# Branch units of a hybrid decoder step: each weight chunk for three token tiles in turn, instead of tile by tile

## The reference, cut to what matters

```python
z = h @ w_in
u, q, k, v, ga, gb = jnp.split(z, IN_SPLITS, axis=-1)
...
br_a = a @ w_a                                # pooling branch, 512 -> 1024
br_b = o.reshape(B, T, ATTN_WIDTH) @ w_b      # attention branch, 512 -> 1024
merged = jax.nn.sigmoid(ga) * br_a + jax.nn.sigmoid(gb) * br_b
x = x + gt1 * (merged @ w_out)
h2 = rms_norm(x, g2) * (1 + sc2) + sh2
x = x + gt2 * (jnp.square(jax.nn.relu(h2 @ w_up)) @ w_down)
```

## Time and profile before

| | |
|---|---|
| median of 3 runs | 1297.88 us |
| lowest and highest | 1294.77, 1298.71 us |
| the profiled execution, own time | 1296.93 us |
| its span, first to last instruction | 1295.1 us |
| TensorE busy | 1272.9 us (98%) |
| VectorE, ScalarE, GpSimd busy | 811.7, 577.8, 191.0 us |
| granted TensorE clock, mean | 0.997 of full |
| branch stage | 425.6 to 518.8 us |

### The profile page before, as it was taken

The page is one execution under the profiler, slowest core; times in us unless marked ns, Lnnn a source line. Parts: engine busy times, 40 slices in busy tenths (PEclk is TensorE's granted clock), DMA queues, the critical chain, the costliest instruction groups (busy, mean ns, idle before and its releaser), DMA issues. The chain is left out here.

```text
span 1295.1 us, 24747 instructions
## 1 busy us (share of the span) xinstructions
PE 1272.9 (98%) x10221; PEld 1246.7 (96%) x10221; DVE 811.7 (63%) x1221; ACT 577.8 (45%) x998; POOL 191.0 (15%) x182
## 2 busy tenths in 40 slices
PE   6999999999999999999999999999999999999997
PEld 5999999999998999999999999999999999999996
DVE  7611446664434655447898877677679885688874
ACT  5412324444344533336765555555563434334252
POOL 1000100000000122222353333232310000000021
PEclk9999999999999999999999999999999999999999
DMA  9988422222222443545336554544498666776533
GB/s 308 329 282 280 151 67 67 66 73 81 79 67 75 163 138 115 152 124 152 104 116 200 166 154 126 166 134 141 153 339 279 206 197 224 214 234 200 184 127 101
DMA packets 239596, 211.59 MB, mean 163 GB/s; under 512 B 17185, under 2 KB 220837, under 8 KB 234605
## 3 DMA queue, kind: packets, MB, share of 16 engines
q1 hardware_dynamic: 238620, 209.66, 51.3%
q10 hardware_dynamic: 865, 0.36, 0.1%
HBM read 161.97 MB, written 49.04 MB: 163 GB/s over the span
## 5 line engine op out<-in xcount | busy, mean ns | idle before, releaser
L588 PE MATMUL psum<-xh,b_lo 128*128 128x264 f32 x908 | 257.7, 284 | 0.0
L586 PE MATMUL psum<-xh,b_hi 128*128 128x264 f32 x908 | 256.8, 283 | 0.8 <-DVE b_lo L1835 0.8
L587 PE MATMUL psum<-xl,b_hi 128*128 128x264 f32 x908 | 256.2, 282 | 0.0
L586 PE MATMUL psum<-dh,e_hi 128*128 128x264 f32 x896 | 254.9, 285 | 0.0
L587 PE MATMUL psum<-dl,e_hi 128*128 128x264 f32 x896 | 253.8, 283 | 0.0
L588 PE MATMUL psum<-dh,e_lo 128*128 128x264 f32 x896 | 253.7, 283 | 0.0
L586 PE MATMUL psum<-h_hi,w_hi 128*128 128x384 f32 (+1 forms) x624 | 208.1, 333 | 1.5 <-issue 1.5
L587 PE MATMUL psum<-h_lo,w_hi 128*128 128x384 f32 (+1 forms) x624 | 201.7, 323 | 0.0
L588 PE MATMUL psum<-h_hi,w_lo 128*128 128x384 f32 (+1 forms) x624 | 201.4, 323 | 0.0
L586 PEld LDWEIGHTS psum<-xh,b_hi 128*128 128x128 f32 x908 | 170.5, 188 | 1.1 <-DVE b_lo L1835 1.0
L587 PEld LDWEIGHTS psum<-xl,b_hi 128*128 128x128 f32 x908 | 170.5, 188 | 0.0
(11 more groups left out here) (315 smaller groups left out, 2418.5 us busy)
## 6 DMA issues: line engine op xcount, KB each, us to landing
down_raw<-in_w_down_dram SPq DMA_DIRECT2D x72, 512.0 KB, 5.7
dr<-ff_scratch SPq DMA_DIRECT2D x28, 1056.0 KB, 7.7
up_raw<-in_w_up_dram SPq DMA_DIRECT2D x76, 256.0 KB, 3.8
ff_scratch<-st SPq DMA_DIRECT2D x64, 264.0 KB, 3.2
ada_p<-in_w_ada_dram SPq DMA_DIRECT2D x8, 2048.0 KB, 9.6
ff_scratch<-st SPq DMA_DIRECT2D x32, 396.0 KB, 3.7
w_raw<-in_w_in_dram SPq DMA_DIRECT2D x22, 512.0 KB, 5.0
gates_scratch<-g_out SPq DMA_DIRECT2D x16, 528.0 KB, 3.2
```

Source lines behind the costliest of these rows:

```text
L586: mm(out, whi, rhi, start=first, stop=False)
L587: mm(out, whi, rlo, start=False, stop=False)
L588: return mm(out, wlo, rhi, start=False, stop=last)
```

## The change

All eight units now go by chunk: chunk 0 for the three tiles, chunk 1 for the three, and so on. Unit 0 keeps its order of the branches, a then o; the others keep o then a. Only TensorE's stream is edited; the other engines' programs are as they were.

```diff
-                if j == 0:
-                    for b0, xhi, xlo, c0 in ((0, a_hi, a_lo, 0), (3, o_hi, o_lo, 4)):
-                        for k in range(4):
+
+                both = ((0, a_hi, a_lo, 0), (3, o_hi, o_lo, 4))
+                for b0, xhi, xlo, c0 in both if j == 0 else both[::-1]:
+                    for k in range(4):
+                        if j == 0:
                             pe.wait_ge(s_lo_done, S_ORDER.index(c0 + k) + 1)
-                            for t in range(3):
-                                if k == 0:
-                                    wait(pe, free[b0 + t], take(b0 + t, ("ab", j, b0 // 3, t)))
-                                last = mm3(psum[:, b0 + t, 0:TW[t]], whi[:, c0 + k, :], wlo[:, c0 + k, :], xhi[:, k, cols(t)], xlo[:, k, cols(t)], k == 0, k == 3)
-                                if k == 3:
-                                    last.then_inc(ready[b0 + t], 1)
-                    last_of[u] = ("ab", j, 1, 2)
-                    continue
-                for t in range(3):
-                    tile(("ab", j, 1, t), 3 + t, t, u, o_hi, o_lo, range(4, 8))
-                    tile(("ab", j, 0, t), t, t, u, a_hi, a_lo, range(4))
+                        for t in range(3):
+                            if k == 0:
+                                wait(pe, free[b0 + t], take(b0 + t, ("ab", j, b0 // 3, t)))
+                            last = mm3(psum[:, b0 + t, 0:TW[t]], whi[:, c0 + k, :], wlo[:, c0 + k, :], xhi[:, k, cols(t)], xlo[:, k, cols(t)], k == 0, k == 3)
+                            if k == 3:
+                                last.then_inc(ready[b0 + t], 1)
+                    last_of[u] = ("ab", j, b0 // 3, 2)
```

## The result

| | before | changed |
|---|---|---|
| median | 1297.31 us (4 runs) | 1312.88 us (4 runs) |
| lowest and highest | 1294.77, 1298.71 | 1310.79, 1315.40 |
| profiled execution, own time | 1296.93 | 1315.40 |
| its span | 1295.1 | 1313.6 |

The ratio is 1.0125, with a 95% interval of 1.0113 to 1.0136: slower by 15.6 us in the medians. The forecast was 1314.3 us, with a range of 1308 to 1321, and its sum was +16.4 us.

The account below looks back on a forecast made before the run. TensorE alone was taken to bound the kernel. Waits of 2.27 us behind unit 0, 11.5 behind units 1 to 6 and 2.60 before the output stage made +16.4 us, forecasting 1314.3 us against the median, range 1308 to 1321.

Parts of the forecast that it names:

- The bound and the pace: Branch stage: TensorE alone sets its length; matmul pace unchanged by chunk order, 11.70 us a unit against 11.62.
- The rival of a faster or slower pace: Chunk order is faster on TensorE, winning back 16.4 us, 0.033 us per step, in seven units; chance of faster 0.01.
- Demand and supply of bank 5: Between units: bank 5 wanted at E + 1.05, but o2, behind a0 and `mg_low(0)` on VectorE, ends at E + 2.75.
- Behind unit 0: Seam from unit 0 to unit 1: TensorE's seventh matmul waits for bank 5, a loss of 2.27 us.
- The six like seams: Seams behind units 1 to 6: TensorE waits for bank 5, 1.92 us each, 11.5 us in all.
- E: The moment when one unit's last matmul has gone through TensorE and the next unit may start.
- Before the output projection: Behind unit 7: the first output tile waits for `mg_low` of unit 7, tile 0, a loss of 2.60 us.
- The clock: At the new waits: no fall, as they are shorter than the earlier one; rival of falls, 3.4 to 13.6 us, chance 0.12.
- if a stretch at the lower clock follows the waits: Sign of being wrong: TensorE runs at the lower clock behind the new waits; the forecast expected granted clock 1.00.
- What was covered: Behind a2: next weights covered by 4.9 us, gates' load covered, output stage's own loads without loss.
- the first rival: Longer seams: slow `mg_low(0)` and GpSimd sum at every seam add 5.9 us, giving 1320.2; chance 0.10.

Follow-up runs that it names:

- e1_o_first: Changed kernel, with VectorE emptying o0, o1, o2 before a0, a1, a2 in units 1 to 7: 1303.99 us.
- e2_mg_low_late: Changed kernel, with every `mg_low` on VectorE placed behind a2, the o and a order kept: 1300.71 us.
- e4_a_first: Changed kernel, with the branches in the order a, o in all units on TensorE, VectorE's order kept: 1322.20 us.
- e5_all_waits_gone: Changed kernel, with VectorE emptying the first-filled branch first, GpSimd waiting for both products, the output projection waiting for unit 7's `mg_low` only before its last chunk: 1298.65 us.
- e6_only_unit1: Kernel before, with the chunk order added in unit 1 alone: 1298.99 us.
- e3_last_by_tile: Changed kernel, with unit 7 done tile by tile again: 1308.69 us.

## Why the prediction was right

**The bound and the pace.** Right. With the waits taken out, units in chunk order last 11.63 us (e1_o_first), against 11.62 in the tile order. The rival of a faster or slower pace had 0.01 of the chances and deserved no more.

**Demand and supply of bank 5.** Right in place and mechanism: the wait is at the seventh matmul, and it goes when o2 is taken out ahead (e1_o_first) and nearly so when `mg_low(0)` stands behind it (e2_mg_low_late). It grows when the last bank wanted is freed later (e4_a_first: 2.66 us, 2.6 expected).

**The terms.** The sum was 2.27 + 6 x 1.92 + 2.60 = 16.4. In the changed kernel's trace:

- Behind unit 0 bank 5 opens at 440.69; with this execution's 0.13 us later start of the stage it would have opened at 438.62: 2.07, and 0.07 for the restart: 2.1.
- The six like seams follow each other at 13.37 to 13.39 us (505.68 - 492.31 = 13.37): 1.76 each, not 1.92. The restart was taken as 0.15 us from the earlier trace rows, where it is 0.06 here, and a0 starts at E - 0.72 instead of E - 0.66. This term is off by 1.0 in all.
- Before the output projection: `mg_low(7, 0)` ends at 535.44, the matmul starts at 535.54, and E was 533.16: 2.38, with the restart 2.5.

Together 15.2 us where 16.4 were forecast.

**The clock.** This step was wrong: "I take no fall." In the profiled execution it fell twice, and with that one of the forecast's own signs of being wrong was met, "if a stretch at the lower clock follows the waits"; the others were not. The first fall cost 1.5 us, the second 1.7 (the output stage and all behind it took 778.06 instead of 776.32 us, less 0.08 of restart). 15.2 + 1.5 + 1.7 = 18.4, and 0.1 for the later start of the stage: this is what the execution is longer than that of before (1315.40 - 1296.93 = 18.5). The four times of the changed kernel are 13.5 to 18.1 us above the 1297.31 of before; the low end is 1.7 below the sum without falls, within the spread that the kernel before has itself, and the upper end needs the falls. So two errors ran against each other: waits taken 1.2 us too long in all, and falls left out (by difference 0.4 us in the median, which is 15.6 above that of before, and 3.2 in the profiled execution). That they had opposite signs is luck; the waits alone, 15.2 us, would have been inside the range too.

The Trainium skill (TensorE: Matmul & The Clock Gate, "A second HAM failure mode: psum-queue depth-cycling") had the direction right: waits between groups of matmuls, each for a bank, did bring stretches at half clock. The forecast let the dense work around the waits speak against it. In this kernel the effect stays a side cost, falls of 1.5 to 1.7 us beside 15.2 us of plain waiting.

**What was covered.** The weights (`w_lo`), the gates and the output stage's loads were on time, as argued: no wait on them appears in the changed kernel. The longer seams of the first rival did not come: `mg_low(0)` took 0.72 to 0.78 us, and a pair of GpSimd sums 1.95 to 1.97, at all seams alike.

## What to carry to other kernels

Before several banks are filled in turn instead of one after another, write down when each is wanted again and where it stands in the order of the engine that empties it. The price is that difference at each seam, and it is decided by what stands ahead of the last bank wanted, here a step that itself waits for two other engines; the remedy that keeps the chunk order is in the emptying engine's order (e1_o_first, e2_mg_low_late), while another order of the branches on TensorE made it worse (e4_a_first). A wait that is taken away uncovers the next one behind it (e5_all_waits_gone), and here a wait of about two microseconds on TensorE cost, in some executions, nearly as much again in clock.

## What was not expected of the hardware

The clock falls at waits much shorter than the 2.93 us of the earlier trace rows, and not each time. Counted over the profiles: at the seam of unit 0 with `mg_low(0)` ahead of o2 it fell in three of four (the changed kernel, e1_o_first, e6_only_unit1; not e3_last_by_tile). There TensorE had been held for about 0.2 us at bank 4 and then issued nothing from 438.95 to 440.69. At the last wait, 2.4 us, it fell in two of three (not in e2_mg_low_late), besides the longer one of e4_a_first. At the eleven seams of 1.76 us in the changed kernel and e3_last_by_tile, with nothing issued for 1.66 us, it never did. But in e4_a_first, where the longest stretch without a matmul is as short (1.65 us) and stands behind waits of 0.5 and 0.2 us, it fell at three seams of seven. So it is not the length of the one wait alone. What decides between a fall and none at the same seam these runs do not tell; a fall cost 1.5 to 1.7 us each time.
